# A two-block transformer kernel: 17 pieces of the conditioning matrix summed on VectorE, all pieces as units of 512 columns

## What is computed

```python
c_act = jax.nn.silu(c)
mod = c_act @ w_ada + b_ada                      # [2048] x [2048, 12288]
sh1, sc1, gt1, sh2, sc2, gt2 = jnp.split(mod, 6, axis=-1)
h = modulate(rmsnorm(x, g_norm_mix), sh1, sc1)   # h * (1 + sc1) + sh1
proj = h @ w_in                                  # three parts of 1024 columns: xr, gr, xp
xr = causal_dwconv(xr, w_conv, b_conv)
hr = rg_lru(xr, ...)                             # two gates, then a scan over time
y_lru = hr * gelu(gr)
y_pool = pool_mixer(xp, w_pool, ls_pool)         # moving averages over 2, 4, 8, 16 tokens, less x
x = x + gt1 * (concat(y_lru, y_pool) @ w_out)
h = modulate(rmsnorm(x, g_norm_ffn), sh2, sc2)
x = x + gt2 * ((silu(h @ w_gate) * (h @ w_up)) @ w_down)
```

## Time and profile before

| | |
|---|---|
| three runs, median (lowest, highest) | 2598.79 us (2597.09, 2599.3) |
| the profiled execution | 2601.92 us |
| its span | 2600.1 us |
| mean granted TensorE clock | 0.988 |
| TensorE busy (matmul) | 2534.6 us, 97% |
| VectorE busy | 1780.3 us, 68% |
| ScalarE busy | 1183.7 us, 46% |
| GpSimd busy | 58.0 us, 2% |
| DMA | 554.51 MB, mean 213 GB/s |

### The profile page before, as it was taken

One profiled execution on the slowest core, in us unless ns is written; L12 is line 12 of the kernel. 1 busy time (PEld: TensorE's weight loads), 2 busy tenths in 40 slices (PEclk: granted clock), 3 DMA queues, 4 the chain that ended last, 5 costly groups with the idle time before them and its releaser, 6 DMA issues.

```text
span 2600.1 us, 40492 instructions
## 1 busy us (share of the span) xinstructions
PE 2534.6 (97%) x14844; PEld 2169.0 (83%) x14844; DVE 1780.3 (68%) x2298; ACT 1183.7 (46%) x1444; POOL 58.0 (2%) x108
## 2 busy tenths in 40 slices
PE   5999999999999999999999999999999999999998
PEld 3776688888888888888888888888888888888887
DVE  3556688955555555688686565676788668875886
ACT  3345335444444444564454554455544444444444
POOL 1211000000000000000000000000000000000000
PEclk8999999999999999999999999999999999999999
DMA  9988997955555556566555555555555655555554
GB/s 377 367 314 290 358 370 259 358 171 191 187 190 187 188 186 193 161 196 201 191 168 172 164 173 190 186 185 194 176 182 191 201 187 188 184 193 179 193 165 126
DMA packets 158859, 554.51 MB, mean 213 GB/s; under 512 B 16400, under 2 KB 20496, under 8 KB 158752
## 3 DMA queue, kind: packets, MB, share of 16 engines
q1 hardware_dynamic: 142192, 491.12, 56.2%
q0 software_dynamic: 16560, 61.94, 6.6%
HBM read 550.37 MB, written 2.10 MB: 212 GB/s over the span
## 4 chain that ended last, share of the span: by engine, by line
PE 83%; DVE 4%; ACT 2%; DMA 1%; issue 1%; DVEq 0%; ACTq 0%
PE ps L600 51%; PE ps L607 25%; PE ps L597 2%; DVE split L1293 1%; PE ps L604 1%; DMA ride<-in_w_ada 1%; DVE acc_out L1350 1%; DMA add_out<-in_w_ada 1%; ACT split L957 1%; PE pm L638 0%; DVE x_t L1446 0%; DVE val L1303 0%; PE pm L662 0%; PE pm L763 0%; DVE h_s L1641 0%
## 5 line engine op out<-in xcount | busy, mean ns | idle before, releaser
L1293 DVE TENSOR_TENSOR split<-raw,split 128x1024 fp32r<-128x1024 f32 (+1 forms) x864 | 1030.5, 1203 | 709.2 <-ACT split L957 705.9
L957 ACT ACTIVATE split<-raw 128x1024 fp32r<-128x1024 f32 (+1 forms) x864 | 896.4, 1043 | 1156.1 <-PE ps L607 1017.0
L600 PE MATMUL ps<-h_s,split 128*128 128x512 f32 x3624 | 1147.2, 398 | 5.1 <-DVE h_s L1424 2.5
L607 PEld LDWEIGHTS ps<-h_s,split 128*128 128x128 f32 x3624 | 682.8, 188 | 161.7
L600 PE MATMUL ps<-mid_s,split 128*128 128x512 f32 x2336 | 736.5, 397 | 0.5 <-DVE split L1293 0.4
L607 PE MATMUL ps<-h_s,split 128*128 128x256 f32 x3624 | 713.8, 278 | 0.0
L600 PEld LDWEIGHTS ps<-h_s,split 128*128 128x128 f32 x3624 | 555.0, 189 | 15.3 <-issue 10.1
L607 PEld LDWEIGHTS ps<-mid_s,split 128*128 128x128 f32 x2336 | 439.4, 188 | 104.0
L607 PE MATMUL ps<-mid_s,split 128*128 128x256 f32 x2336 | 459.4, 278 | 0.0
L600 PEld LDWEIGHTS ps<-mid_s,split 128*128 128x128 f32 x2336 | 356.3, 189 | 9.8 <-issue 7.8
L963 ACT ACTIVATE low<-ps 128x512 f32<-128x512 f32 x214 | 123.9, 579 | 0.0
(11 more groups left out here) (275 smaller groups left out, 1376.7 us busy)
## 6 DMA issues: line engine op xcount, KB each, us to landing
raw<-in_w_in SPq DMA_DIRECT2D x224, 512.0 KB, 3.5
raw<-in_w_ffn_down SPq DMA_DIRECT2D x128, 512.0 KB, 4.2
ride<-in_w_ada POOLq DMA_DIRECT2D x56, 1024.0 KB, 9.7
raw<-in_w_ffn_gate SPq DMA_DIRECT2D x88, 512.0 KB, 3.4
raw<-in_w_ffn_up SPq DMA_DIRECT2D x88, 512.0 KB, 3.5
raw<-in_w_ffn_a SPq DMA_DIRECT2D x88, 512.0 KB, 4.2
raw<-in_w_ffn_b SPq DMA_DIRECT2D x88, 512.0 KB, 4.4
raw<-in_w_out SPq DMA_DIRECT2D x64, 512.0 KB, 4.3
```

The lines of the kernel that those rows point to most:

```text
L600: pe.matmul(ps[:, s, b, :], split[:, slot, k, 0, b * P:(b + 1) * P], acts[:, k0 + k, :, :].rearrange("p h t -> p (h t)"), start=start, sto ...
L607: mm = pe.matmul(ps[:, s, b, 0:T], split[:, slot, k, 1, b * P:(b + 1) * P], acts[:, k0 + k, 0, :], start=False, stop=stop)
L957: act.activation(split[:, c, 0:kt, 0, :], raw[:, CHUNKS * s + c, 0:kt, :], ACT.Copy).then_inc(hi_ready, 1)
L1293: dve.tensor_tensor(split[:, c, 0:kt, 1, :], raw[:, CHUNKS * s + c, 0:kt, :], split[:, c, 0:kt, 0, :].bitcast(F32), ALU.subtract).then_inc ...
```

## The change

All of TensorE's w_ada work becomes units of 512 columns and four pieces: 16 units (g = 0 to 15) instead of eight units and four parts. The pieces stay 64, of 1 MB each, at the same chunks. A part's turn becomes two, so turns lie at G = 28, 32, 36, 40, 44, 48, 60 and 72. Seventeen of the 56 later pieces go to VectorE: in each of passes 0, 1 and 2 piece 3 of the even unit (at q = 1) and pieces 1 and 3 of the odd one (q = 3 and 4); later pieces 1 and 3 of units 8, 9 and 13 and piece 3 of units 10 and 12 (G = 25, 27, 29, 31, 35, 43, 45, 47). VectorE sums such a piece into one buffer `unit_acc` in four operations. A unit with such pieces is turned by eight matmuls instead of four: each block of `row` with `sel` and of `unit_acc` with `ones` into the same PSUM column. The slot of such a piece is free once VectorE has summed it (`unit_added`). `windows(2)` moves from chunk 37 to 34 and `windows(3)` from 42 to 35.

```diff
-WINDOWS_AT = (32, 33, 37, 42)
+WINDOWS_AT = (32, 33, 34, 35)
+VECTOR_LATE = {8: (1, 3), 9: (1, 3), 10: (3,), 12: (3,), 13: (1, 3)}
 def _rides():
-    at = [PASS_SLABS * p + c for p in range(CHUNKS - 1) for c in (0, 0, 1, 1, 3, 3, 4, 4)]
+    for p in range(CHUNKS - 1):
+        g = PASS_SLABS * p
+        at += [(g, False), (g, False), (g + 1, False), (g + 1, True)]
+        at += [(g + 3, False), (g + 3, True), (g + 4, False), (g + 4, True)]
...
+    unit_acc = at("unit_acc", [P, 512], F + 45152)
...
+    def load_ada(queue, piece):
+        slot, _, last = ada_place(piece)
+        if last in VECTOR_PIECES:
+            queue.wait_ge(unit_added, vector_count(last))
+        elif last >= 0:
+            queue.wait_ge(ada_multiplied, tensor_count(last))
...
         def turn_ada(g):
             pe.wait_ge(row_copied, g + 1)
+            both = unit_vector(g)
+            if both:
+                pe.wait_ge(unit_added, vector_count(UNIT_PIECES * g + UNIT_PIECES - 1))
             for j in range(4):
+                to, block = pm[2 + g % 2][:, j:j + 1], slice(j * P, (j + 1) * P)
+                mm = pe.matmul(to, row[:, block], sel[:, 0:1], start=True, stop=not both)
+                if both:
+                    mm = pe.matmul(to, unit_acc[:, block], ones[:, 0:1], start=False, stop=True)
             mm.then_inc(ada_turned, 1)
...
+        def sum_unit(piece):
+            g, i = divmod(piece, UNIT_PIECES)
+            src = ada_slot(ada_place(piece)[0])
+            done = vector_count(piece) - 4
+            dve.wait_ge(*landed(piece))
+            if piece == min(p for p in VECTOR_PIECES if p // UNIT_PIECES == g):
+                earlier = [p // UNIT_PIECES for p in VECTOR_PIECES if p // UNIT_PIECES < g]
+                if earlier:
+                    dve.wait_ge(ada_turned, earlier[-1] + 1)
+                dve.tensor_scalar(unit_acc[:, :], src[:, 0, :], c_act[:, 4 * i:4 * i + 1], None, ALU.mult).then_inc(unit_added, 1)
+                first = 1
             else:
+                first = 0
+            for e in range(first, 4):
+                dve.wait_ge(unit_added, done + e)
+                dve.scalar_tensor_tensor(out=unit_acc[:, :], in0=src[:, e, :], scalar=c_act[:, 4 * i + e:4 * i + e + 1],
+                                         in1=unit_acc[:, :], op0=ALU.mult, op1=ALU.add).then_inc(unit_added, 1)
         def finish_rides(G):
             for g, at in LAST_RIDE.items():
                 if at + 1 == G:
                     finish_ada(g)
+            for piece, at, vector in RIDES:
+                if at == G and vector:
+                    sum_unit(piece)
```

More of the change, by code:

```diff
@@ L266, in ada_place, with tensor_count, vector_count, unit_vector @@
         if piece < first_late:
-            return piece % UNIT_RING, piece // UNIT_RING + 1, piece - UNIT_RING + 1
+            return piece % UNIT_RING, piece // UNIT_RING + 1, piece - UNIT_RING
         slot, turn = (piece - first_late) % LATE_RING, (piece - first_late) // LATE_RING
         before = first_late // UNIT_RING
-        last = piece - LATE_RING if turn else first_late - UNIT_RING + slot
-        return slot, before + turn + 1, last + 1
+        return slot, before + turn + 1, piece - LATE_RING if turn else first_late - UNIT_RING + slot
+    def tensor_count(piece):
+        return sum(p <= piece for p in TENSOR_PIECES)
+    def vector_count(piece):
+        return 4 * sum(p <= piece for p in VECTOR_PIECES)
+    def unit_vector(g):
+        return any(p // UNIT_PIECES == g for p in VECTOR_PIECES)
+    def landed(piece):
+        slot, times, _ = ada_place(piece)
+        if piece < 2 * UNIT_PIECES:
+            return ada_loaded[slot], 16 * times
+        return ada_pooled[slot], 16 * (times - 2 * UNIT_PIECES // UNIT_RING)
     def pass_sum(q):
@@ L423, in build @@
     block = ctx.enter_context(nc.Block())
[L426 to L439, removed]
+    def load_ada(queue, piece):
[5 more added lines that the diff above has]
+        g, i = divmod(piece, UNIT_PIECES)
+        src = dram["w_ada"][4 * i * P:4 * i * P + 4 * P, _column(g):_column(g) + 512].rearrange("(k p) n -> p k n", p=P)
+        queue.dma_start(ada_slot(slot), src).then_inc(landed(piece)[0], 16)
     @block.sync
@@ L457, in _ @@
         for piece in range(UNIT_PIECES):
-            load_ada(sp, ada_loaded, piece)
+            load_ada(sp, piece)
         for G in range(2):
@@ L544, in _ @@
         pool.wait_ge(constants, 3)
-        for piece in range(2 * UNIT_PIECES, UNITS * UNIT_PIECES + TENSOR_PARTS * PIECES):
-            load_ada(pool, ada_pooled, piece)
+        for piece in range(2 * UNIT_PIECES, ALL_UNITS * UNIT_PIECES):
+            load_ada(pool, piece)
             if piece == 4 * UNIT_PIECES:
@@ L665, in ride_along @@
         def ride_along(G):
-            for r, at in enumerate(RIDE_AT):
-                if at == G:
-                    multiply_ada(2 * UNIT_PIECES + r)
+            for piece, at, vector in RIDES:
+                if at == G and not vector:
+                    multiply_ada(piece)
             for g, at in LAST_RIDE.items():
```

88 lines of the change are left out of this document (34 added, 54 removed).

## The result

| | before | after |
|---|---|---|
| median of the runs beside each other | 2597.94 us (2596.43 to 2599.3, 4 runs) | 2634.81 us (2627.52 to 2638.92, 4 runs) |
| ratio after / before | | 1.0139, 95% interval 1.0114 to 1.0164 |
| the profiled execution, its span, mean granted clock | 2601.92, 2600.1, 0.988 | 2627.52, 2625.7, 0.981 |

The change makes the kernel slower by 37 us where +16 was forecast; the measured median lies above the range of 2593 to 2628. The profiled execution of after is the quickest of its four, so its trace shows 25.6 of the 33 to 37 us.

The account below looks back on a forecast made before the run. TensorE was taken to set the pace, its idle time being the possible gain. Terms +5.6 (passes 0 to 2), +2.3, +3.9, +3.7 and +0.9 (OUT turn) gave +16.4 us on 2598.79: 2615 us, range 2593 to 2628.

Parts of the forecast that it names:

- Pieces and turns: TensorE's exchanged work: seventeen pieces less, -16.2 us, against longer and extra turns, +13.5 us; its own work falls under 3 us.
- The sums and, in passes 1 and 2, the waits behind them: VectorE sums of 2.6 and 2.9 us per piece; TensorE waits 1.7 us in even units, 3.6 in odd.
- Rivals A and B: A: VectorE takes over TensorE's landing waits, 2579 us, chance 0.16; B: stalls only replace landing waits, 2600 to 2603, 0.14.
- eleven times: Expected sign: TensorE waits for unit_acc at the turns' second matmul group, 1.5 to 4 us each, eleven times.
- 2 x (1.7 + 2.6): Passes 1 and 2: cost of an even plus an odd unit, twice, +8.6 us; less 2.0 of landing waits, +6.6.
- rival C: New waits make TensorE's clock slow; the four longest cost 2 us each more: +24, 2623 us, chance 0.12.
- Pass 0: Three landing waits pass to VectorE; TensorE runs on one chunk, then waits twice and pays two longer turns: -1.0 us.
- Pass 3 and slab 8: Units 8 to 10, late pieces on VectorE: +2.3 us, taken by the ring.
- The ring of two slots: Pass 3: slot 1's cycle of landing, sum, next issue takes 9.8 to 11.2 us against 9.8; three cycles 0 to +4.2.
- Chunk 35: Surest term: unit 10's sum and windows(3) come before the evacuation, so all behind it is 4 us later: +3.9 us.
- Chunks 38 to 49: Units 11 to 13: +0.6 us at chunk 43 and +3.1 at chunk 47, where the load is issued later; +3.7 us.
- The two-port rule: VectorE's two-port mode blocks GpSimd's DMA descriptors; eleven products by a scalar: up to 4.4 us more, left out of the sum.

Follow-up runs that it names:

- the version without waits: Against the changed kernel: one VectorE piece per unit of the passes, sums before conversions, no late pieces, moving averages at old places; 2600.86 us, ratio 1.0011.
- fill run: The changed kernel plus 16 or 30 unused matmuls before each turn of the passes, where TensorE would wait for unit_acc; 2621.74 us, ratio 1.0082.
- second profile: Profile of the second timing of the changed kernel, same program; that execution took 2635.93 us, the timing's median 2631.39 us, ratio 1.012.
- the version with sums first: The changed kernel with VectorE's unit sums ahead of the conversion in the passes and slabs 8 to 11, same 17 pieces; 2604.73 us, ratio 1.0025.

## Why the prediction was wrong

The direction and the place were right, the size was not.

**Pieces and turns: right.** A piece was put at 0.95 and the longer turn at +0.9; they measure 0.97 and 1.70 against 0.81. That TensorE's own work hardly falls was the firm point, and it is why even the version without waits gains nothing.

**The sums and, in passes 1 and 2, the waits behind them: right to within 0.4 us.** The first piece of a unit and a later one on VectorE in pass 1 of after:

```profile
99.36 0.49 DVE L1352 TENSOR_SCALAR unit_acc<-ride,c_act 128x512 f32<-128x512 f32 x1
99.89 2.33 DVE L1358 SCALAR_TENSOR_TENSOR unit_acc<-ride,c_act,unit_acc 128x512 f32<-128x512 f32 x3
...
117.40 3.11 DVE L1358 SCALAR_TENSOR_TENSOR unit_acc<-ride,c_act,unit_acc 128x512 f32<-128x512 f32 x4
```

That is 2.9 and 3.1 us for a forecast of 2.6 and 2.9. The even turns wait 2.08 us (1.7), the odd ones 3.84 and 3.61 (3.6). Rivals A and B fell with this: in the passes no sum ended before TensorE was there. Later three of five did (the turns at chunks 28, 32 and 44 do not wait), so "eleven times" was eight.

**What failed is the price of a wait in the passes.** The term for two units was "2 x (1.7 + 2.6)", wait and work alone, and the clock was a rival with a chance of 0.12 and a price of "2 us each" for the four longest waits. Pass 2 grew by 10.05 us, from 34.66 to 44.71. The forecast has 3.3 of them (1.7 + 2.6 less 1.0 of landing waits). The rows have 1.25 us more in the chunk behind the even turn (4.36 less 3.11), 1.62 in the odd turn (3.40 less the 1.78 that such a turn takes at full speed) and 2.46 in the two chunks behind it (8.45 less 5.99), 5.3 in all; the longer even wait gives 0.4 and the landing wait of 0.62 that stood for 1.0 another 0.4. Less than 1 us is open. The fill run says the same from the other side, 10 us for six turns. So rival C had the right mechanism, with too few waits in it. Its condition was misjudged in one point: only the four longest waits were given a price, since a piece behind 2.23 us was still quick. In after, both waits of 2.08 us, followed by a turn and not by a piece, left a slow chunk behind, and a piece behind 1.98 us was slow itself. "TensorE: Matmul & The Clock Gate" of the Trainium skill says in its part on the clock gate that idleness throttles the array; the trace agrees (a granted clock of 0.50 behind 3.61 us of wait, and 8.45 us for two chunks).

**Pass 0: wrong in sign, and not steady.** Forecast -1.0. The first pieces behind chunk 8 start at 90.33 us before and at 91.29 in after, +0.6 if chunk 0 is set equal; in the second profile at 95.18, +5.3, through one wait of 5.51 us. VectorE's waiting for a landing does not free TensorE; it puts the sum behind it.

**Pass 3 and slab 8: half of it, for a wrong reason.** +4.4 for +2.3. The ring of two slots was named as the cause. The rows show two gate products waiting 3.85 and 2.06 us for xc behind a unit sum; behind the longer wait the gates and the chunk after them take 2.8 us more than before (a chunk of 4.41 instead of 3.22). With the turn at chunk 28 (+1.8), four pieces less (-3.9) and the landing wait of 1.8 us that is gone, this makes +4.8. That place was missed because the order of VectorE was read at chunk 35 and not at the gates.

**Chunk 35: partly there.** The stretch gave +2.9 for +3.9, and windows(3) away from chunk 35 shortened it by 1.7 us. The work was priced rightly and set against a TensorE that was on time; it no longer was. The "about 8 us" of waiting for mid_s at chunk 37 was 1.54. And "that the two leave chunks 37 and 42 gives nothing" was true of the kernel before; with a sum at chunk 43 it is worth about what they cost at chunk 35.

**Chunks 38 to 49: too high.** +0.6 for +3.7. TensorE waits 1.83 us for a landing at 290.13 us, where it had 2.23, and 4.72 us for unit_acc at the turn at 313.60, where it had 4.08 for a landing. One wait took the place of another.

**The two-port rule was not tested.** By the Trainium skill's "SBUF — State Buffer", on the trap that VectorE blocks DMA, the ride issues should lengthen beside the products by a scalar. In the passes they take 751 ns at the median and 902 at most in after, and took 748 and 899 before; but no ride issue of after runs at the same time as one of the eleven products (0.48 to 0.51 us each), so the trace neither bears the rule out nor speaks against it. Leaving it out of the sum cost nothing.

## What to carry over

Where TensorE sets the pace, price a new wait by what stands on both sides of it: add to the wait the thin matmuls next to it and some microseconds at half speed behind them, as soon as the trace shows such a wait with a slow row after it. Before work is moved to a half-idle engine, look where in its order the result stands: the change with the same 17 sums costs 33 to 37 us behind the conversion and 6 ahead of it. And count what handing the result back costs; here a turn longer by 0.9 us ate the piece of 0.97 that was saved. Nor is a microsecond saved on TensorE won when its next operand comes from a load that is already the later of the two.

## What was not expected of the hardware

A wait of 2.08 us leaves TensorE at 2.4 GHz when dense matmuls follow (24 in 3.11 us). When a turn of one-column matmuls follows, 1.77 us long, part of the next chunk runs at 1.2 GHz (it takes 4.36). That the turn is what makes the difference is likely but not shown. The same kind of turn without a wait costs nothing behind it in the version with one piece in each unit (3.11 and 5.99). It is not fully regular: with the wait filled, one such chunk in pass 2 still took 4.61 us, and in the version with sums first waits of 1.81 and 1.67 us ahead of like turns were followed by 7.97 and 5.99 us for two chunks. What tells these cases apart stays open. And 17.5 us of matmuls that nothing reads (three times 2.08 and three times 3.76 us) made the kernel 10 us faster.
